# The even layer of an encoder step as 72 tile steps, each with attention of one head group and one projection job of the next

## What is computed

```python
def even_mixer(h, w_in, w_out, lam, out_scale, subln_g, relb, t5_a, ...):
    aq, ak, av, bq, bk, bv = split_cols(h @ w_in, (A_W, A_W, A_W, B_W, B_W, B_W))   # 6 x 512 columns
    oa = diff_attend(aq, ak, av, t5_bias, chunk_visible, lam)   # 4 heads, two maps each: softmax_0 - lam * softmax_1
    ob = band_prompt(bq, bk, bv, B_LEFT, clipped_bias)          # 8 heads of width 64, at most 9 chunks of 64 keys
    oa = rms_norm(oa, subln_g) * out_scale
    mix = concatenate([oa, ob], -1)                             # 1024 wide
    return mix @ w_out, new_a, new_b                            # new keys and values are outputs too
```

## Time and profile before

| | us |
|---|---|
| median of 3 runs (3517.25 to 3524.36) | 3521.65 |
| the profiled execution, its own time | 3521.4 |
| its span, first to last instruction | 3519.6 |
| even layer in it: first projection to the first matmul of LayerNorm | 90.5 to 893.1 |

### The profile page before, as it was taken

One profiled execution on the slowest core, in us unless ns is written; L12 is line 12 of the kernel. 1 busy time (PEld: TensorE's weight loads), 2 busy tenths in 40 slices (PEclk: granted clock), 3 DMA queues, 4 the chain that ended last, 5 costly groups with the idle time before them and its releaser, 6 DMA issues.

```text
span 3519.6 us, 49427 instructions
## 1 busy us (share of the span) xinstructions
PE 3046.1 (87%) x18006; PEld 2812.2 (80%) x18153; DVE 1512.5 (43%) x3607; ACT 935.9 (27%) x2258; POOL 832.2 (24%) x425
## 2 busy tenths in 40 slices
PE   1788889888699999999876777689996999999996
PEld 1777778888599999999754565578876999999994
DVE  1445543444522322332438888843543322232233
ACT  2444444444411011101232222244443101101113
POOL 0122122111133243334101111012112343334330
PEclk8899999999899999999967666699998999999998
DMA  5111011111011111111000001010000111111101
GB/s 120 40 44 44 26 46 40 39 33 31 18 48 42 42 48 47 48 36 54 15 11 17 16 16 29 1 33 22 21 19 24 42 48 48 42 42 48 48 30 49
DMA packets 197964, 128.80 MB, mean 37 GB/s; under 512 B 24435, under 2 KB 180403, under 8 KB 197875
## 3 DMA queue, kind: packets, MB, share of 16 engines
q1 hardware_dynamic: 185104, 121.87, 11.5%
q10 hardware_dynamic: 12770, 5.79, 1.1%
HBM read 110.28 MB, written 17.34 MB: 36 GB/s over the span
## 4 chain that ended last, share of the span: by engine, by line
PE 69%; DVE 15%; ACT 6%; issue 6%; ACTq 1%; DMA 1%; another core or an unknown queue 1%; POOL 1%; SPq 0%; DVEq 0%; POOLq 0%; PEldq 0%
PE ps L734 19%; PE ps L735 19%; PE ps L736 19%; PE ps L846 5%; DVE sel_mask L1396 4%; PE ps L758 3%; DVE Y L1566 2%; ACT xf L1270 2%; PE ps L958 1%; DVE yc L1623 1%; PE ps L1032 1%; PE ps L809 1%; PE ps L811 1%; DVE sd L1621 1%
## 5 line engine op out<-in xcount | busy, mean ns | idle before, releaser
L734 PE MATMUL ps<-Xh,w_hi 128*128 128x352 f32 (+1 forms) x3024 | 990.9, 328 | 126.2 <-PEq L919 77.5
L735 PE MATMUL ps<-Xl,w_hi 128*128 128x352 f32 (+1 forms) x3024 | 978.9, 324 | 0.0
L736 PE MATMUL ps<-Xh,w_lo 128*128 128x352 f32 (+1 forms) x3024 | 978.5, 324 | 0.0
L631 POOL TENSOR_TENSOR w_hi<-w_raw,zero 128x1024 fp32r<-128x1024 f32 x186 | 351.5, 1890 | 2558.6 <-PE ps L736 1261.6
L734 PEld LDWEIGHTS ps<-Xh,w_hi 128*128 128x128 f32 (+1 forms) x3024 | 574.6, 190 | 131.4 <-issue 62.8
L735 PEld LDWEIGHTS ps<-Xl,w_hi 128*128 128x128 f32 (+1 forms) x3024 | 575.4, 190 | 0.5
L736 PEld LDWEIGHTS ps<-Xh,w_lo 128*128 128x128 f32 (+1 forms) x3024 | 573.5, 190 | 0.5
L633 POOL TENSOR_TENSOR w_lo<-w_raw,w_hi 128x1024 fp32r<-128x1024 f32 x186 | 449.3, 2416 | 14.6
L1659 DVE TENSOR_TENSOR hid_f<-ps,gate_s 128x352 f32<-128x352 f32 x132 | 69.3, 525 | 811.8 <-PE ps L736 811.8
L1666 DVE TENSOR_TENSOR Y<-ps,Y 128x352 f32<-128x352 f32 x528 | 274.5, 523 | 212.7 <-PE ps L736 212.7
L734 PE MATMUL ps<-Hh,w_hi 128*128 128x352 f32 x1056 | 343.7, 325 | 9.9 <-DVE Hl L1661 9.9
(11 more groups left out here) (224 smaller groups left out, 3974.3 us busy)
## 6 DMA issues: line engine op xcount, KB each, us to landing
w_raw<-in_w_ffn_in_dram SPq DMA_DIRECT2D x176, 256.0 KB, 3.1
w_raw<-in_w_ffn_out_dram SPq DMA_DIRECT2D x88, 256.0 KB, 2.8
w_raw<-in_w_in_even_dram SPq DMA_DIRECT2D x48, 256.0 KB, 3.9
w_raw<-in_w_in_odd_dram SPq DMA_DIRECT2D x26, 256.0 KB, 3.4
x_in<-in_x_prompt_dram SPq DMA_DIRECT2D x8, 512.0 KB, 7.5
w_raw<-in_w_out_even_dram SPq DMA_DIRECT2D x16, 256.0 KB, 2.8
w_raw<-in_w_out_odd_dram SPq DMA_DIRECT2D x16, 256.0 KB, 3.7
out_dram<-Y SPq DMA_DIRECT2D x8, 512.0 KB, 2.9
```

The costliest lines, as they stand in the source:

```text
L631: pool.tensor_tensor(view(WH[w][:, :]), raw, zeros, ALU.add).then_inc(S["w_split"], 1)
L734: pe.matmul(out, wh, hi, start=first, stop=False)
L735: pe.matmul(out, wh, lo, start=False, stop=False)
L736: return pe.matmul(out, wl, hi, start=False, stop=last)
```

## The change

The stages of "AB" are replaced by one phase, EV, written out without loops, in `even_layer` of each engine.

- There are 72 steps n, nine tiles t for each of eight groups g ("AAAABBBB"). In a step TensorE runs the two scores of tile n, the first two transpose groups of tile n-1, projection job n+9, a side group (key, cache or output transposes), what transposes are left, and the value products of tile n-1. ScalarE and VectorE have the order shown below. The first group's nine jobs stand ahead of the steps.
- A group's nine jobs: K in chunks of 384, 384 and 288 columns, V, Q. K and Q as before, V now with the tokens on partitions (four tiles, four, and the sample tile): x is the stationary operand and 128 weight columns stream, so that V's transposes go. In the steps all jobs write PSUM bank 7; the transposes have two banks, the values one, the scores four.
- Keys, values and bias are in two slots. Probabilities are in a ring of two. Transposes always take 128x128.
- There is no down part. A group's outputs are transposed and split in the steps of the group after (t = 5 to 7), and for the first six groups parked in DRAM. At the end they are loaded into Xh and Xl, and 24 jobs of 24 matmuls with the full depth of 1024 follow (five banks), added to Y by VectorE.
- Y gives its memory to the key slots: the setup writes ALPHA * x through four staging buffers to DRAM (18 DMAs of SP, ScalarE waiting for the buffer of four groups before), and two DMAs bring it back in the eighth group.
- GpSimd waits for the phase's barrier before its first split of EV; before, that split was ahead of the barrier. SP loads weights, cache rows and bias rows a group ahead.

The core of the diff, by engine.

Layout and the side groups:

```diff
-STAGES = {"A0": (1, None, None, "A", 0, True), "AL": (3, "A", 0, "A", 1, True),
-          "AE": (1, "A", 3, "B", 0, True), "BL": (3, "B", 0, "B", 1, True), "BE": (1, "B", 3, None, None, False),
+EV_KINDS = "AAAABBBB"
...
+EV_STEPS = TILES * len(EV_KINDS)
+EV_CHUNKS = [(0, 3 * P), (3 * P, 3 * P), (6 * P, T - 6 * P)]
...
+EV_HEAD_BANKS = [7, 0, 1, 2, 3]
...
+def side_group(n):
+    g, t = n // TILES, n % TILES
+    if t in (1, 2, 3) and g < EV_LAST and key_tiles(EV_KINDS[g + 1], t - 1):
+        return ("k", g + 1, t - 1)
+    if t == 4 and g < EV_LAST:
+        return ("cache", g + 1, 0)
+    if t in (5, 6, 7) and g > 0:
+        return ("o", g - 1, t - 5)
...
+        def e_tbank(key):
+            return ps[:, 4 + EV_T[key] % 2, :].rearrange("p (j c) -> p j c", j=4)
+        def e_job_bank(j):
+            return ps[:, EV_HEAD_BANKS[j % 5] if j < TILES else 7, :]
```

SP, in the setup:

```diff
+                for g in range(X_GROUPS):
+                    sp.wait_ge(S["setup_xh"], g + 1)
...
+                    sp.dma_start(y_park[:, 4 * half:4 * half + 4, t * P:t * P + nq], ystage[:, g % 4, :, 0:nq]).then_inc(S[f"e_yst{g % 4}"], 16)
```

GpSimd:

```diff
+            def even_layer():
+                before("EV", "pool", pool)
...
+                split(0)
+                split(1)
+                fill_bias(0)
+                split(2)
+                split(3)
+                for g in range(EV_LAST):
+                    split(3 * g + 4)
+                    fill_bias(g + 1)
+                    split(3 * g + 5)
+                    split(3 * g + 6)
```

TensorE, a job, with the form of V:

```diff
+                def job(j):
+                    q, i = j // TILES, j % TILES
+                    u = 3 * q + i // 3
+                    if i % 3 == 0:
+                        ready(ev, u)
+                    old = (j - 5 if j >= 5 else None) if j < TILES else (5 if j == TILES else j - 1)
+                    if old is not None:
+                        name, n = job_done(old)
+                        pe.wait_ge(S[name], n)
...
+                        for t in TM_ALL[i - 3]:
+                            rows = DEC if t == NT else P
+                            out = bank[0:rows, t % 4 * P:t % 4 * P + P]
+                            for k in range(KB):
...
+                                pe.matmul(out, xh, wh, start=(k == 0), stop=False)
+                                pe.matmul(out, xl, wh, start=False, stop=False)
+                                mm = pe.matmul(out, xh, wl, start=False, stop=(k == KB - 1))
```

TensorE, the steps:

```diff
+                for n in range(EV_STEPS + 1):
+                    groups = len(prob_blocks(n - 1)) if n else 0
+                    if n < EV_STEPS:
+                        score(n, 0)
+                        score(n, 1)
+                    for k in range(min(2, groups)):
+                        prob_transposes(n - 1, k)
+                    if n + TILES < EV_STEPS:
+                        job(n + TILES)
+                    if n < EV_STEPS:
+                        side(n)
+                    for k in range(2, groups):
+                        prob_transposes(n - 1, k)
+                    for k in range(groups):
+                        values(n - 1, k)
```

TensorE, the output projection:

```diff
+                for o in range(3 * KB):
+                    u = 3 * len(EV_KINDS) + o // 3
+                    if o % 3 == 0:
+                        ready(ev, u)
+                    if o >= 5:
+                        pe.wait_ge(S["e_y"], o - 4)
+                    c = o % 3
+                    for k in range(KB):
+                        mm = three(ps[:, EV_HEAD_BANKS[o % 5], 0:CH], e_unit_slot(u), k, Xh[:, k, c * CH:(c + 1) * CH],
+                                   Xl[:, k, c * CH:(c + 1) * CH], k == 0, k == KB - 1)
```

ScalarE, the steps:

```diff
+                for n in range(EV_STEPS + 1):
+                    groups = len(prob_blocks(n - 1)) if n else 0
+                    for k in range(min(2, groups)):
+                        prob_rows(n - 1, k)
+                    if n < EV_STEPS:
+                        exps(n)
+                    if n + TILES < EV_STEPS:
+                        job(n + TILES)
+                    if n < EV_STEPS:
+                        side(n)
+                    for k in range(2, groups):
+                        prob_rows(n - 1, k)
+                    if n:
+                        output_rows(n - 1)
```

VectorE, the steps:

```diff
+                for n in range(EV_STEPS):
+                    maxima(n)
+                    if n % TILES == 1 and n > TILES and EV_KINDS[n // TILES - 1] == "A":
+                        normed(n // TILES - 1)
+                    weights(n)
+                    if n + TILES < EV_STEPS:
+                        job_low(n + TILES)
+                    side(n)
```

More of the change, by code:

```diff
@@ L149 @@
                relu=4 * N_IDX, acc=4 * N_IDX, dve=N_IDX - 1)
[L151 removed]
+SETUP_INC = dict(w_split=4, d_done=36, act_ev=1, dve_ev=6, pv=1, soft=1, onorm=1, stores=16)
 X_GROUPS = 2 * (NT + 1)
[L153 to L158 removed]
[2 rows of a table removed]
+SETUP_PART = dict(tgroups=X_GROUPS, units=2, jobs=36, act_ev=1, dve_ev=6, pv=1, soft=1, onorm=1, stores=16)
@@ new lines, with key_tiles, prob_blocks @@
+EV_KINDS = "AAAABBBB"
+EV_LAST = len(EV_KINDS) - 1
+TILES = NT + 1
+EV_STEPS = TILES * len(EV_KINDS)
+EV_CHUNKS = [(0, 3 * P), (3 * P, 3 * P), (6 * P, T - 6 * P)]
+EV_TILES = [[0, 1, 2], [3, 4, 5], [6, 7, NT]]
+EV_BLOCKS = P_MAPS["B"] * -(-(5 * P) // P)
+EV_PART = dict(units=3 * len(EV_KINDS) + KB, jobs=TILES * len(EV_KINDS) + 3 * KB)
+EV_HEAD_BANKS = [7, 0, 1, 2, 3]
+def key_tiles(kind, c):
+    return [t for t in EV_TILES[c] if kind == "A" or t >= 4]
+def prob_blocks(n):
+    kind = EV_KINDS[n // TILES]
+    nk = tile_spec(kind, n % TILES)[3]
+    blocks = [(m, j) for m in range(P_MAPS[kind]) for j in range(len(key_blocks(nk)))]
+    return [blocks[a:a + 4] for a in range(0, len(blocks), 4)]
@@ new lines, in side_group, with transpose_order @@
+def side_group(n):
[6 more added lines that the diff above has]
+        return ("o", g - 1, t - 5)
+    return None
+def transpose_order():
+    order = [("k", 0, c) for c in range(3)] + [("cache", 0, 0)]
+    for n in range(EV_STEPS + 1):
+        groups = range(len(prob_blocks(n - 1))) if n else []
+        order += [("p", n - 1, k) for k in groups if k < 2]
+        if n < EV_STEPS and side_group(n):
+            order.append(side_group(n))
+        order += [("p", n - 1, k) for k in groups if k >= 2]
+    return order + [("o", EV_LAST, k) for k in range(3)]
@@ L571, in load_ffn @@
+            even_layer()
             def load_ffn(l):
@@ L700, in mixers, with even_layer, split, settled @@
                     stage(name, pool, stage_splits)
-            mixers("AB")
+            def even_layer():
+                before("EV", "pool", pool)
+                for n in range(2):
+                    pool.memset(eV[n][:, NT + PAST // P, :], 0.0).then_inc(S["e_zero"], 1)
+                    pool.memset(eO[:, n, NT, :], 0.0).then_inc(S["e_zero"], 1)
+                units = 3 * len(EV_KINDS)
+                steps = [0]
+                def split(u):
+                    n, slot = BASE["EV"]["units"] + u, e_unit_slot(u)
+                    pool.wait_ge(w_loaded[slot], n // 2 * 32)
+                    if u >= 2:
+                        old = u - 2
+                        pool.wait_ge(S["d_done"], e_jobs(3 * (old + 1)))
+                    raw = w_raw[:, slot, :]
+                    pool.tensor_tensor(WH[slot][:, :], raw, zero[:, 0:1].to_broadcast([P, D_MODEL]), ALU.add).then_inc(S["w_split"], 1)
+                    pool.wait_ge(S["w_split"], n * 2 + 1)
+                    pool.tensor_tensor(WL[slot][:, :], raw, WH[slot][:, :].bitcast(F32), ALU.subtract).then_inc(S["w_split"], 1)
+                def settled(ins):
+                    steps[0] += 1
+                    ins.then_inc(S["e_pool"], 1)
+                def mask(part, p0):
+                    pool.wait_ge(S["e_pool"], steps[0])
+                    z = zero[p0:p0 + HD, 0:1].to_broadcast([HD, HD])
+                    n = neg[p0:p0 + HD, 0:1].to_broadcast([HD, HD])
+                    settled(pool.tensor_tensor(part, z, n, ALU.add))
+                def fill_bias(q):
+                    kind = EV_KINDS[q]
+                    width = WINDOW[kind] * P
+                    pool.wait_ge(S[f"e_bld{q % 2}"], 16 * sum(B_MAPS[k] for k in EV_KINDS[q % 2:q + 1:2]))
+                    for m in range(B_MAPS[kind]):
+                        rows = e_bias(q, m)
+                        if steps[0]:
+                            pool.wait_ge(S["e_pool"], steps[0])
+                        far = rows[:, width - NEAR:width - NEAR + 1].to_broadcast([P, width - NEAR])
+                        settled(pool.tensor_tensor(rows[:, 0:width - NEAR], zero[:, 0:1].to_broadcast([P, width - NEAR]), far, ALU.add))
+                        mask(rows[0:HD, width - HD:width], 0)
+                        if kind == "B":
+                            mask(rows[HD:P, 0:HD], HD)
+                    pool.wait_ge(S["e_pool"], steps[0])
+                    pool.sem_inc(S["e_bok"], 1)
```

(8 more changed lines are left out.)

506 lines of the change are left out of this document (493 added, 13 removed), and 1 row of the table STAGES.

## The result

The changed kernel takes 3526.91 us (median of 20 runs, 3519.53 to 3530.41), the kernel before 3518.67 us beside it (20 runs): a ratio of 1.0022, interval 1.0015 to 1.0029. It is slower by 8 us where 16 us less were forecast. The profiled execution has a span of 3523.3 us.

What follows compares the result with a forecast made beforehand. TensorE bounds the V steps; in-order softmax, copies and low parts around single bank 7 pace most others. The even layer ends at 856.5 against 893.1 us (-36.6); additions leave net -16, so 3505, range 3450 to 3560.

Steps and rivals of the forecast that it cites:

- the term for the V steps: Tiles 3 and 4 of each group, with the long V jobs: 23.5 (A) or 24.2 us (B), TensorE-bound.
- the sign: What the changed profile would show: groups of 79 to 81 us, with 10 to 13 us of TensorE idle in each.
- V's own price: Token-major V projection: 11 us more per group, 87 in all, against 72 V transposes saved (8 us).
- The third rival: Loads of V's matmuls hide under the matmul before: up to 80 us go, at the middle 3465; chance 0.07.
- The setup: Ahead of the first projection: 90.5 us before, plus 16 for stores and 5.4 for GpSimd's later first splits.
- the stores' part of it: 18 stores of scaled residual ahead of the barrier: 20 us per engine, barrier moved by 0 to 20, 16 taken.
- K and Q steps: Tiles 0 to 2 and 6 to 8: 20.7 us for K; 27.0 (A) or 28.3 (B) for Q.
- Tile 5 of the A groups: Step with only the sample tile's V: 8.1 us from scores, maxima, exponentials, map difference and output low part.
- The splits: GpSimd's weight splits hold up VectorE's negation: 15 us over 64, half of it on the chain, 8.
- The eighth group: Last head group, without jobs: VectorE goes M, E, M (maxima, exponentials, maxima), 38 us; 5 more for half clock.
- The slower rival: TensorE falls to 1.2 GHz in K and Q steps: 3.9 us more per step, a third of them 3560; chance 0.2.
- The rival that the overlap buys nothing: Whole kernel: stores cost 20 us, the additions 32 instead of 20, so 3521; chance 0.15.

Runs made afterwards that it cites:

- the first run: The changed kernel with the third of V's three products (high x times low weights) left out: 3463.3 us, ratio 0.9841.

## Why the prediction was wrong

- **The step that failed** is the term for the V steps, "21.1 of job plus 2.4 (A) or 3.1 (B) of scores, transposes and values between them: 23.5 or 24.2". From the first maximum of tile 3 to that of tile 5 there are two jobs and two sets of other work, and I took one. Measured: 21.5 of jobs plus 6.2 (A) or 7.3 (B). The bound was right (TensorE; the first run shows it one for one), the size off by 4.2 and 4.6 us: 4 x 4.2 + 3 x 4.6 = 31 us, more than the whole miss of 24 at the end of the even layer. The one set was short as well: the prediction has as many value products as transposes, "41 or 70 of each", but the earlier trace rows show 16 beside 8 transposes, and the timeline of the third A group has 8 for the tile whose transposes are 4; that is 0.3 or 0.4 us of a set in A. The group's own total of TensorE work, 66 or 71 us, is short for the same reason: with 82 or 140 value products it is 70.5 or 78.7. Less 45.4 for the nine jobs, that leaves 2.8 or 3.7 us for each tile, and two of them beside the jobs' 21.1 would have given 26.7 and 28.5, most of the miss. The windows bear it out: TensorE is idle for 9 us of an A group and 3 of a B group, where 10 to 13 were named as the sign, and one group took 89 us, over the 86 that were named as wrong.
- **V's own price held.** 11 us more a group was forecast from 0.11 us a matmul; the trace has 0.112, and the kernel with V undone is 85 us faster in all, where 87 less 8 for the transposes was the sum. It comes back as 13 us in the two long steps, less 2 to 3 in tile 5 and, in B groups, 1 to 2 in tile 6, in each of seven groups, and 10.5 in the first group's own jobs. The third rival, hidden loads, is out. The Trainium skill (TensorE: Matmul & The Clock Gate, Back-to-back issue gap) has 81 ns for that shape; this trace, with 112, does not agree.
- **The setup held in size, the stores' part of it by luck**: 110.9 for 111.9. The barrier moved by 15 us where 16 were taken, and the splits cost 5.2 where 5.4 were. The 16 were 20 us of engine time with 4 of it hidden; the stores took 13.5, and the 15 show nothing of that hidden. The price of 35 ns for a packet was the wrong unit, as the packed stores show: by bytes the same row gives 14 us (121.87 MB in 405 us of each engine, 4.3 MB of stores). Nor does the barrier still wait for the table's write, which is only 6 us late: it waits for the stores behind it. By the Trainium skill (DMA: Bandwidth & Descriptors, Why a DMA increments its semaphore by 16 and not by 1) a transfer uses the largest number of engines up to 16 that divides the slowest dimension of both its sides, so that the stores' whole time would come on top of a table's write on 8 engines; 13.5 and 15 us are near that, but the runs do not separate that rule from the row's flat pace.
- **K and Q steps held** by the formula (longer of the two chains), the step's handoffs included: the 7 us set aside for those were not needed. **Tile 5 of the A groups is luck**: of its 8.15 us for 8.1, 1.7 are the split, which the formula does not hold; without splits it takes 6.47, and in B groups 6.3 for 7.5. Without splits the seven groups take 578 us, 21 over the 557: the V steps' 31, less 10 by which the other lines are shorter than worked out, most of it in tile 5.
- **The splits** cost 14 us in the groups, not 8, all of it in the A groups: each is released by a job's end at a fixed place of the step, so it hits the same operation every time. In the second and fourth A group 1.5 us of it each are the clock, as told below.
- **The eighth group** took 48.3 us, not 41, and the 5 us set aside there for half clock were not needed for that (granted clock 0.99). "VectorE goes M, E, M" gives 3.6 us a tile of 640 keys; such tiles take up to 6.0 in it, with transposes, their two copies and 20 value products of 0.11 us in turn on the chain. This was read from the chain, not tested.
- **The slower rival**, 1.2 GHz in the K and Q steps, did not decide: the groups have a granted clock of 0.96 to 1.00. But its mechanism is real and near. One split moved onto the chain brought it in for 13 us a group. In the second and fourth A group of the changed kernel it is there in small: tile 6 takes 11.3 us instead of 9.8. Windows at the end of tile 5 and the start of tile 6 in the fourth:

```profile
470.00:476.00 6.00, 3.36 (x24) 2.88 (x22) 3.85 (x8) 3.27 (x9) 4.18 (x2) 1.00 0.17 48
476.00:480.00 4.00, 4.00 (x17) 3.76 (x15) 2.53 (x9) 2.20 (x5) 0.00 (x0) 0.58 0.35 131
```

- **The rival that the overlap buys nothing** came nearest in time (3521), for another reason. Of the 106 us that the seven groups lost, some 81 are the down part (24 x 3 x 0.16 us a group by the earlier trace rows, an estimate), which the output projection has now. With V as before and the parks first the seven groups take 521 us, 178 less than in the kernel before; so the overlap itself is worth some 97 us, and V's form takes 72 of them back in the groups and 10.5 ahead of them.

## What to carry to other kernels

When steps repeat, count from one event to the same event of a later step, and check the sum of the steps against the engine's total work; a stretch of two steps has two of everything. Count an operation in a row of the trace, not from the plan: here the rows had two value products for each transpose. An edit that saves transposes by making the moving side narrow is paid in more matmuls, here of 0.112 us for 128 columns where a wide one takes 0.058 for as many: price it by the pace of that very shape in the trace. Before moving a release (a split, a store) in a program that an engine runs in order, name the operation that it will fall on at its new place, and what TensorE does while that waits.

## What was not expected of the hardware

- A GpSimd split does not slow VectorE evenly. The negation, the small products and the difference of two maps in memory wait until it ends (0.17 to 1.78, 0.16 to 1.53, and 0.62 to 2.59 us for a difference of 384 columns); the maxima, which read PSUM (0.69 us for 512 columns either way), and the reciprocal (0.17) went on beside it. The Trainium skill (SBUF — State Buffer, Who interferes with whom) has the two engines share a port pair that one takes for a whole instruction, in some forms of VectorE's operations; the rows agree.
- At 1.2 GHz a V matmul of 128 columns follows the one before after 0.21 us, and a V job of 20 us, without a gap, ran at that clock but for its first 0.7 us. The timeline of the run with K jobs on three banks:

```profile
399.50 0.41 PE L1274 MATMUL ps<-w_hi,Xl 128*128 128x128 f32 x1
399.72 0.41 PE L1275 MATMUL ps<-w_lo,Xh 128*128 128x128 f32 x1
```

The windows above show 2.4 GHz again only after the scores that follow the job. In the changed kernel the fall at 476 us, before a Q job of 384 columns, was over by 480.
